# Down-projection chunks with two neighbouring rows to a partition, and the matching stride of four columns in the hidden transposes

## What is computed

```
logits = h @ w_router + b_router            # 320 x 32
top_v, top_e = top_k(logits, 4); gate = softmax(top_v)
for each expert e, for the rows that chose it:
    hu  = x @ w_up[e] + b_up[e]             # 1024 -> 2048
    g   = min(hu[:, 0::2], 7.0)             # even columns: gate
    u   = clip(hu[:, 1::2], -7.0, 7.0)      # odd columns: up
    act = (u + 1) * g * sigmoid(1.702 * g)  # 1024
    y   = act @ w_down[e] + b_down[e]       # 1024 -> 1024
out[row] += gate * y
```

## Time and profile before

| | us |
|---|---|
| median of 3 runs (lowest, highest) | 1650.87 (1649.14, 1663.3) |
| the profiled execution | 1654.17 |
| its span | 1652.4 |
| DVE busy | 1239.3 (75%) |
| PE busy | 1402.2 (85%) |
| ACT busy | 939.2 (57%) |
| granted TensorE clock, mean | 0.916 |

### The profile page before, as it was taken

The page is one execution under the profiler, slowest core; times in us unless marked ns, Lnnn a source line. Parts: engine busy times, 40 slices in busy tenths (PEclk is TensorE's granted clock), DMA queues, the critical chain, the costliest instruction groups (busy, mean ns, idle before and its releaser), DMA issues.

```text
span 1652.4 us, 21727 instructions
## 1 busy us (share of the span) xinstructions
PE 1402.2 (85%) x6257; PEld 997.2 (60%) x6258; DVE 1239.3 (75%) x1254; ACT 939.2 (57%) x864; POOL 295.6 (18%) x416
## 2 busy tenths in 40 slices
PE   5993586989988999999899999999988998999660
PEld 3762465654537667666676666667766766767440
DVE  0245564755548999999889999999988898898745
ACT  0011323602116877887678878877767776787522
POOL 5302989820300001000100101001000000000000
PEclk8997787659898999999999999999999999999885
DMA  9975364052418999999989999999988999899734
GB/s 350 364 246 155 91 209 170 1 152 81 161 37 320 384 405 395 393 407 398 367 318 404 395 401 389 393 406 398 397 314 335 383 407 369 325 403 406 260 129 150
DMA packets 124955, 498.52 MB, mean 302 GB/s; under 512 B 21106, under 2 KB 46275, under 8 KB 91027
## 3 DMA queue, kind: packets, MB, share of 16 engines
q1 hardware_dynamic: 104146, 454.56, 71.6%
q0 software_dynamic: 14768, 29.16, 5.2%
q10 hardware_dynamic: 5984, 14.11, 2.4%
HBM read 499.43 MB, written 26.25 MB: 318 GB/s over the span
## 4 chain that ended last, share of the span: by engine, by line
PE 42%; DVE 25%; issue 15%; ACT 8%; SPq 6%; DMA 3%; DVEq 1%; ACTq 0%; POOL 0%; POOLq 0%
PE psum L537 39%; DVE w_lo L1789 14%; SPq L391 4%; ACT w_hi L1243 4%; PE psum L540 3%; ACT arena L1203 2%; DMA early<-in_pages 1%; DVE arena L1812 1%; DMA arena<-y_dram 1%; DVE arena L1814 1%; DVE x_split L1844 1%; DVE arena L1433 1%; DVE arena L1434 1%; DVE arena L1335 1%; DMA arena<-in_w_down 1%
## 5 line engine op out<-in xcount | busy, mean ns | idle before, releaser
L1789 DVE TENSOR_TENSOR w_lo<-arena,w_hi 128x2048 fp32r<-128x2048 f32 x352 | 795.4, 2287 | 107.9 <-ACT w_hi L1243 107.3
L1243 ACT ACTIVATE w_hi<-arena 128x2048 fp32r<-128x2048 f32 x344 | 652.9, 1913 | 238.1 <-PE psum L537 233.9
L537 PE MATMUL psum<-arena 128*128 128x64 f32 (+10 forms) x2194 | 464.9, 385 | 41.0 <-DMA arena<-in_w_in 18.7
L537 PE MATMUL psum<-w_hi,x_split 128*128 128x512 f32 x1628 | 441.0, 399 | 14.8 <-DVE x_split L1844 6.0
L537 PE MATMUL psum<-w_lo,x_split 128*128 128x512 f32 x1408 | 401.5, 407 | 58.8 <-DVE w_lo L1789 53.9
L537 PEld LDWEIGHTS psum<-arena 128*128 128x128 f32 (+3 forms) x2194 | 300.4, 194 | 205.6 <-issue 157.7
L537 PEld LDWEIGHTS psum<-w_lo,x_split 128*128 128x128 f32 x1408 | 255.1, 190 | 171.6 <-DVE w_lo L1789 124.8
L537 PEld LDWEIGHTS psum<-w_hi,x_split 128*128 128x128 f32 x1628 | 305.7, 191 | 79.6 <-issue 12.5
L2003 POOL DMA_INDIRECT y_dram<-y_part,arena x32 | 38.4, 1199 | 1004.2 <-DVE y_part L1850 731.0
L540 PE MATMUL psum<-arena 128*128 128x128 f32 (+4 forms) x581 | 96.2, 320 | 84.3 <-ACT arena L1087 30.0
L540 PEld LDWEIGHTS psum<-arena 128*128 128x128 f32 (+4 forms) x581 | 79.2, 167 | 103.6 <-issue 42.5
(11 more groups left out here) (229 smaller groups left out, 750.7 us busy)
## 6 DMA issues: line engine op xcount, KB each, us to landing
arena<-in_w_up SPq DMA_DIRECT2D x256, 1024.0 KB, 7.6
arena<-in_w_down SPq DMA_DIRECT2D x128, 1024.0 KB, 7.2
early<-in_pages SPq DMA_DIRECT2D x160, 128.0 KB, 2.7
arena<-in_w_in ACTq DMA_DIRECT2D x23, 512.0 KB, 7.3
arena<-in_pages POOLq DMA_DIRECT2D x32, 128.0 KB, 7.0
early<-in_pages POOLq DMA_DIRECT2D x32, 128.0 KB, 6.4
arena<-in_pages SPq DMA_DIRECT2D x32, 128.0 KB, 2.2
early<-in_w_plg SPq DMA_DIRECT2D x1, 4096.0 KB, 14.5
```

The costliest lines, as they stand in the source:

```text
L537: return TE.matmul(out, lhsT, rhs, start=start, stop=stop, skip_group_check=True)
L1243: SE.activation(w_hi[:, (8 + t) % 3], chunk_in[(8 + t) % 6], ACT.Copy).then_inc(hi_ready, 1)
L1789: VE.tensor_tensor(w_lo[:, at], chunk_in[buf], w_hi[:, at].bitcast(f32), SUB).then_inc(lo_ready, 1)
```

## The change

The two rows of w_down that share a partition in a chunk are now neighbours (rows 2p and 2p+1 of the 256), where they were 128 apart (rows p and p + 128). A partition then gets 8 KB in one piece, where it got two pieces of 4 KB. The contraction must meet the same hidden units, so block 2q+a of the turned hidden units now holds units 256q + 2p + a. In `hu`, gate and up alternate, so the columns of a block lie four apart, where they lay two apart, and start at 512 (j // 2) + 2 (j % 2) + s. The bias `b_up` is laid out on the host to match. No instruction is added or removed on any engine, no semaphore wait is changed, and the shapes of all operands stay.

```diff
-            down = A["w_down"].rearrange("e (k a p) n -> e k p a n", p=128, a=2)
+            down = A["w_down"].rearrange("e (k p a) n -> e k p (a n)", p=128, a=2)
 
             def weights_to(e, c, buf):
 
-                if c < 8:
-                    dst, src = chunk_in[buf], up[e, c] if isinstance(e, int) else up[bass.ds(e, 1), c].rearrange("e p n -> (e p) n")
-                else:
-                    dst = chunk_in[buf].rearrange("p (a n) -> p a n", a=2)
-                    src = down[e, c - 8] if isinstance(e, int) else down[bass.ds(e, 1), c - 8].rearrange("e p a n -> (e p) a n")
-                sp.dma_start(dst, src).then_inc(w_here[buf], 16)
+                of, k = (up, c) if c < 8 else (down, c - 8)
+                src = of[e, k] if isinstance(e, int) else of[bass.ds(e, 1), k].rearrange("e p n -> (e p) n")
+                sp.dma_start(chunk_in[buf], src).then_inc(w_here[buf], 16)
...
+            def hidden_columns(s, j):
+
+                first = 512 * (j // 2) + 2 * (j % 2) + s
+                return hu[:, first:first + 4 * 127 + 1:4]
...
-                            last = turn(psum[:, to + j // 4, (j % 4) * CAP:(j % 4 + 1) * CAP], hu[:, 2 * j * 128 + s:2 * (j + 1) * 128:2])
+                            last = turn(psum[:, to + j // 4, (j % 4) * CAP:(j % 4 + 1) * CAP], hidden_columns(s, j))
...
-                            cols = hu[:, 2 * j * 128 + s:2 * (j + 1) * 128:2]
-                            last = mm(psum[:, 6 + s, j * HALF:(j + 1) * HALF], cols, folder, True, True)
+                            last = mm(psum[:, 6 + s, j * HALF:(j + 1) * HALF], hidden_columns(s, j), folder, True, True)
...
-        b_up=a["b_up"][0].reshape(NE, 8, 128, 2).transpose(2, 0, 3, 1).reshape(128, NE, 16),
+        b_up=a["b_up"][0].reshape(NE, 4, 128, 2, 2).transpose(2, 0, 4, 1, 3).reshape(128, NE, 16),
```

## The result

The changed kernel takes 1797.61 us (median of 4 runs, 1789.72 to 1801.7) against 1654.39 us for the kernel before in the same comparison: a ratio of 1.0854, 95% interval 1.0789 to 1.0919. The forecast was 1782 in a range of 1738 to 1806.

The account below looks back on a forecast made before the run. The prediction took the engine loop, not DMA, to bound the weight stream. It added 94 us for loads, 5 for many items, 32 for the clock and 0 for the transfer, giving 1782 us in a range of 1738 to 1806.

Parts of the forecast that it names:

- What bounds the kernel: Experts' weight stream: a loop of TensorE, ScalarE and VectorE tied by three slots sets the 32.3 us period, not DMA.
- Part 1, the transfer: Down chunks in 8 KB pieces: 0.31 to 0.69 us less transfer an item, hidden by waits for TensorE; taken as 0.
- rival E: Weight stream: DMA does set the pace, so larger pieces give 10 to 22 us, 1629 to 1641; chance 0.05.
- Part 2, the loads: Few items' turn: a load at stride four takes 232 ns in place of 118, 94 us over 27 items.
- slack of 0.17 us: Few item's turn: time by which part 3 of `w_hi` is there before VectorE wants it; leaves 3.48 us of 3.65.
- slack of the other path: From turned values to `hidden_rows`: 1.6 us of slack, so its start 2.05 us later, inside the same delay.
- Part 2, the many items: Turns of the 5 many items: the second eight loads cost 0.9 us more each item, 5 us in all.
- three rows: Turn loads at stride two, fp32r matmuls and a VectorE reduction: each 1.75 to 1.84 ns per 16-byte piece of SBUF.
- The rule of the skill: SBUF reads need two hits on a 16-byte line: stride two free, stride four not; it gives no price.
- Part 3, the clock: Clock falls in the turn, slowing the first up chunk behind it: 1.2 us an item, 32 us over 27 items.
- The sum: Whole kernel: 1652.4 + 94 + 5 + 32 - 0 = 1783 us span, 1785 device time, 1782 as median.
- case A: The forecast: each column's load costs a 16-byte piece and the clock falls in the turn; 1782 us, chance 0.56.

Follow-up runs that it names:

- e1: Kernel before with only the new down chunks (8 KB in one piece), turn and bias as before: 1662.16 us, ratio 0.9997.
- e7: Kernel before, but ScalarE makes chunk 10's high part before copying the up product out of PSUM: 1643.35 us, ratio 0.9904.
- e3: Changed kernel, but a few item's turn moves 128 columns behind each load in place of 64: 1754.54 us, ratio 1.0577.
- e10: Changed kernel, but a few item's turn is 16 transposes in place of 16 float32 products, low halves not added: 1645.21 us, ratio 0.9904.
- e4: Changed kernel with the turn's columns three apart: 1749.43 us, ratio 1.0550.
- e5: Changed kernel with the turn's columns eight apart: 1797.26 us, ratio 1.0832.
- e8: Changed kernel, but ScalarE's copy from PSUM puts the columns in the turn's order, so turn loads read neighbours: 1657.30 us, ratio 0.9971.

## Why the prediction was right, step by step

- **What bounds the kernel.** The period that stayed while the DMA share moved was the right thing to read: the transfer alone changed nothing (e1), with the share near 1.00 in both kernels, and a shorter loop ran on the same queues (e7).
- **Part 1, the transfer, 0.** Measured 0.9997 (0.9973 to 1.0022). Right; rival E is out.
- **Part 2, the loads, 232 ns.** Measured 233. The slack of 0.17 us off the longer turn gave 3.48 us an item; with the clock taken out (e3) the period is 35.87, 3.54 more than 32.33. The step that named what is late next also held: part 3 of `w_hi`, then part 3 of `w_lo`. The slack of the other path was read too large. From the first load of the turn to `hidden_rows` it was 5.39 us and is 7.90 (712.58 to 720.48), so 2.5 us more and not 2.05, a slack of 1.2 us and not 1.6; it stays inside the same delay and cost nothing.
- **Part 2, the many items, 0.9 us each.** Wrong: the transposes at stride four cost what they did, so this term of 5 us is 0. The reason given for the price, that a read of SBUF takes 1.75 to 1.84 ns for each 16 bytes, was carried from three rows to all loads. It holds for the loads of float32 products at two, three and four columns apart, and not for a transpose's load (121 ns at four columns, e10). The three rows agree in size, but that one cause stands behind them was only argued, and the transposes speak against it as a general rule. The VectorE row also differs from its two neighbours in what it writes (96 elements for one), and the matmul's 227 ns lie only 14 above what its columns take anyway. So the mechanism for these loads is shown by the strides (e4, e5), not by the three rows, and that 232 came within 1 ns of the measurement is in part luck.
- **The rule of the skill.** The Trainium skill, "SBUF — State Buffer", section "Door 1: The DMA port swizzle", asks for two hits on a line of 16 bytes for full bandwidth (the four float32 that it then gives as a free stride don't go with that, nor with the 233 ns here). For the float32 product's loads the runs agree: hardly anything at two columns (118 against 112 ns), 175 at three, 233 at four. For transposes they differ (121 at four, 109 with neighbours), and there the measurement decides.
- **Part 3, the clock, 1.2 us an item.** Right in kind and in its bounds of 0.7 to 1.8, but too small: 1.66 (e3 against the changed kernel). "Sometimes the clock will be back earlier" did not come about: the low stretch ends at or behind the end of the first up chunk in the item shown, and in all other few items of the trace but the first three of the stream, where it ends 0.1 to 0.4 us before. 27 x 0.46 = 12 us is most of what the forecast missed. That the slow loads cost nothing more at the lower level was right: they span 7.54 us at either (last section).
- **The sum.** 27 x (3.54 + 1.66) = 140 us, against 1797.6 - 1654.4 = 143 measured, and 131 forecast (the other 3.5 us between 1782 and 1797.6 are the two medians of the kernel before). From 131 to 140 it is 12 too few for the clock, 5 too many for the many items, and 2 too few for the longer turns; so the forecast came closer than its terms, by luck: two of its errors had opposite signs. From the first to the last `result_sum` of a few item the traces take 1043.0 us before and 1181.4 (L1851) after, 138 us more, which leaves nothing for the many items. The 3 us between 140 and 143 are inside the spread of the runs.
- **What was to be seen.** Turn loads of 7.4 us (7.54), a period of 37 in case A (37.5), a DMA share under 0.95 (0.86 from 600 to 700 us) and 16384 packets fewer were there. ScalarE's wait grew by 5.35 us, more than the 3.5 to 5 named, since the clock took more. The slices of the page had shown 9, their highest digit, before, so 8 or 9 afterwards tells little; the windows tell it, with a granted clock of 1.00 before and 0.90 after from 600 to 800 us. "Eight transposes about twice as long" was not there.

## What to carry to other kernels

Before a layout is changed for the sake of a transfer, look whether anybody waits for that transfer, and count what the matching access costs the engine that does set the pace; here a gain that nobody waited for bought a read that everybody waited for. The strided operand of a float32 product's weight load is dear from three columns apart; put the stride where it is free (here ScalarE's copy out of PSUM, 602 ns with and without), or use a transpose if the arithmetic allows. In this kernel slow loads with little to move between them lowered the clock, and the loss went on behind them; moving more columns under the same loads gave 43 us back without changing a result.

## What the runs showed of the hardware that was not expected

- A transpose and a float32 product load the same strided columns at very different prices: 109, 120, 115, 121 and 111 ns for a transpose with columns 1, 2, 3, 4 and 8 apart (e8, before, e4, after, e5; medians of a many item's first eight, clock at 1.00); 112, 118, 175, 233 and 238 ns for each of the two loads of a product. The transposes' small rises don't follow the distance. No run tells why.
- With columns four apart a product's load took 233 ns at either clock level; with two apart it depended on the clock. The first few item's turn lies in a stretch at 0.50 in both kernels; with columns two apart a load takes (6.90 - 0.33) / 31 = 212 ns there and 118 at 1.00, with four apart 233 at both. From the timeline and the windows of the kernel before, and then of the changed one:

```profile
518.18 6.90 PEld L537 LDWEIGHTS psum<-arena 128*128 128x128 f32 x32 [2.96 <-issue]
...
518.30:525.00 6.70, 6.70 (x32) 6.70 (x33) 6.27 (x3) 4.00 (x3) 0.00 (x0) 0.50 0.72 270
```

```profile
525.65 7.54 PEld L534 LDWEIGHTS psum<-arena 128*128 128x128 f32 x32 [2.96 <-issue]
...
525.80:533.00 7.20, 7.20 (x32) 7.20 (x32) 6.70 (x3) 3.96 (x3) 0.00 (x0) 0.50 0.71 262
```

- The granted clock fell to the 1.2 GHz level while TensorE was busy without a gap, in the turns of the changed kernel (4.20 of 4.20 us busy before it fell) and with three columns apart; it stayed up over equally slow loads when each moved 128 columns (e3).
- The period of the changed kernel's steady items was 37.5 us, and that of the run with three columns apart (e4) changed from item to item, between 35.2 and 36.1. In four items running, turns in which the clock fell before they were over (loads of 5.99 and 5.94 us, at 626.39 and 697.88) stand in items of 36.0 and 35.9 us, those with loads of 5.68 us (at 662.37 and 733.79) in items of 35.5 and 35.3; but the fifth, with 5.83 us, stands in one of 35.3. What decides in which item the clock falls early is not known.
